# The w_lo subtraction of a split fp32 product moved from VectorE to GpSimd, with GpSimd's program planned by slots

## The reference, cut to what matters

```python
p = (rmsnorm(x, norm_w) * (1.0 + sc) + sh) @ w_in
pc = (rmsnorm(ctx, norm_w) * (1.0 + sc_c) + sh_c) @ w_in
qa, ka, va, za, qkvb, zb, ab = split_in(p)
y_a = diff_post(diff_attend_blocked(q_l, k_all, v_all, lam), subln_w, lam_init, za)
o_b, o_bc = delta_bidirectional(lat_in, ctx_in)
y_b = delta_post(o_b, dn_norm_w, zb)
x = x + gt * (jnp.concatenate([y_a, y_b], axis=-1) @ w_out)
```

## Time and profile before

| what | value |
|---|---|
| runs | 2801.6, 2807.7, 2818.62 us; median 2807.7 us |
| profiled execution, span | 2805.5 us |
| TensorE busy | 2441.5 us, 87% |
| DVE busy | 1479.5 us, 53%, 2582 instructions |
| ACT busy | 840.5 us, 30% |
| POOL busy | 335.5 us, 12%, 685 instructions |

### The profile page before, as it was taken

The page is one execution under the profiler, slowest core; times in us unless marked ns, Lnnn a source line. Parts: engine busy times, 40 slices in busy tenths (PEclk is TensorE's granted clock), DMA queues, the critical chain, the costliest instruction groups (busy, mean ns, idle before and its releaser), DMA issues. The chain is left out here.

```text
span 2805.5 us, 41589 instructions
## 1 busy us (share of the span) xinstructions
PE 2441.5 (87%) x15126; PEld 2006.7 (72%) x15126; DVE 1479.5 (53%) x2582; ACT 840.5 (30%) x1415; POOL 335.5 (12%) x685
## 2 busy tenths in 40 slices
PE   6799999999898989897898798988889898987776
PEld 2377778777776868685776476868777686866775
DVE  1345556473737373745433746475656656565535
ACT  3433232323223232323111533223232323223223
POOL 0001011111102020201100002020111202021100
PEclk9999999999999999998998699999999999998888
DMA  8945352626253544434334244443243444333433
GB/s 324 355 113 153 83 152 62 167 70 173 70 152 91 140 104 126 110 102 147 109 104 151 81 108 119 103 107 101 77 110 78 123 106 107 95 92 112 125 110 110
DMA packets 580888, 345.00 MB, mean 123 GB/s; under 512 B 45090, under 2 KB 544966, under 8 KB 579990
## 3 DMA queue, kind: packets, MB, share of 16 engines
q1 hardware_dynamic: 553430, 300.38, 38.7%
q10 hardware_dynamic: 27120, 42.02, 4.7%
q0 software_dynamic: 208, 0.72, 0.1%
HBM read 312.07 MB, written 31.00 MB: 122 GB/s over the span
## 5 line engine op out<-in xcount | busy, mean ns | idle before, releaser
L1604 PE MATMUL ps<-h_hi,w_hi 128*128 128x512 f32 (+1 forms) x2080 | 846.7, 407 | 49.2 <-DVE w_lo L972 38.1
L1605 PE MATMUL ps<-h_lo,w_hi 128*128 128x512 f32 (+1 forms) x2080 | 780.5, 375 | 0.0
L1606 PE MATMUL ps<-h_hi,w_lo 128*128 128x512 f32 (+1 forms) x2080 | 779.6, 375 | 0.0
L972 DVE TENSOR_TENSOR w_lo<-w_raw,w_hi 128x1024 fp32r<-128x1024 f32 (+1 forms) x332 | 405.4, 1222 | 329.7 <-ACT w_hi L569 270.0
L1604 PEld LDWEIGHTS ps<-h_hi,w_hi 128*128 128x128 f32 x2080 | 407.6, 196 | 166.5 <-issue 64.4
L569 ACT CAST w_hi<-w_raw 128x1024 fp32r<-128x1024 f32 (+1 forms) x332 | 340.6, 1029 | 522.0 <-PE ps L1606 197.5
L1606 PEld LDWEIGHTS ps<-h_hi,w_lo 128*128 128x128 f32 x2080 | 407.1, 196 | 70.0
L1605 PEld LDWEIGHTS ps<-h_lo,w_hi 128*128 128x128 f32 x2080 | 409.4, 197 | 47.9
L1457 POOL TENSOR_SCALAR small<-small 128x4 f32<-128x4 f32 (+3 forms) x51 | 14.0, 274 | 2056.5 <-DVE small L1260 1018.1
L1854 PE MATMUL ps<-h_hi,w_hi 128*128 128x512 f32 (+1 forms) x448 | 169.7, 379 | 56.7 <-DVE w_lo L972 56.7
L972 DVE TENSOR_TENSOR arena<-arena,ps 128x512 f32<-128x512 f32 x160 | 104.1, 684 | 129.5 <-PE ps L1686 128.6
(11 more groups left out here) (187 smaller groups left out, 3164.0 us busy)
## 6 DMA issues: line engine op xcount, KB each, us to landing
w_raw<-in_w_in SPq DMA_DIRECT2D x260, 512.0 KB, 4.6
ada_raw<-in_w_ada SPq DMA_DIRECT2D x148, 512.0 KB, 5.4
w_raw<-in_w_out SPq DMA_DIRECT2D x64, 448.0 KB, 3.7
w_raw<-in_w_ada SPq DMA_DIRECT2D x44, 512.0 KB, 7.0
arena<-decay_rows ACTq DMA_DIRECT2D x16, 512.0 KB, 5.4
m_chunks<-arena SPq DMA_DIRECT2D x16, 512.0 KB, 5.5
arena<-s_chunks SPq DMA_DIRECT2D x16, 512.0 KB, 3.9
x_channel_major<-arena ACTq DMA_DIRECT2D x1, 4096.0 KB, 17.2
```

What stands on the lines that cost most here:

```text
L972: return V.tensor_tensor(o, a, b, op)
L1604: mm(o, w_hi[:, s, k], h_hi[:, kt, t0:], start=kt == 0, stop=False)
L1605: mm(o, w_hi[:, s, k], h_lo[:, kt, t0:], start=False, stop=False)
L1606: last = mm(o, w_lo[:, s, k], h_hi[:, kt, t0:], start=False, stop=kt == KT - 1)
```

## The change

split_lo goes from the DVE's program to POOL's, with the same operands and semaphores, as a tensor_tensor of POOL. All 332 subtractions go: the two and the one at each layer's start, those of slot 2, 6, 10 and so on of each body, those of the output product, and three of the last four units (the first of these belongs to the output body). POOL's body is now planned by slots as the others are: the power of q and k in slot 3, the products with the gates in slot 6, the memsets in slot 9, the forward substitution in five parts of three steps in slots 15 to 19, the output norms' powers in slot 36 (20 in layer 1) and 58. A subtraction stands ahead of what else is in its slot, in the output body behind it. TensorE's, ACT's and SP's programs are the same as before. On the DVE of layer 1 the modulation of the first 8 and the second 8 channel tiles is now one call, since no subtraction is between them.

```diff
@@ -1015,13 +1015,6 @@
                 vec.wait_ge(diag_ready, n + 1)
                 own.settle()
 
-            def split_lo(i, u, tiles=HALF):
-
-                vec.wait_ge(w_hi_ready, i * UNITS + (u + 1))
-                need(vec, w_used, i * UNITS + (u - 1))
-                tt(w_lo[:, u % 2, 0:tiles], w_raw[:, u % 4, 0:tiles], w_hi[:, u % 2, 0:tiles].bitcast(F32),
-                   ALU.subtract).then_inc(w_split, 1)
-
             def modulate(layer, ks):
 
 
@@ -1060,8 +1053,6 @@
                     rms(0, 0)
                 if g == 2:
                     vec.wait_ge(rms_copied, 1)
-                if g == 7:
-                    split_lo(0, 0)
                 q = modulated_after(g)
                 if q >= 0:
                     modulate(0, range(4 * q, 4 * q + 4))
@@ -1071,14 +1062,9 @@
                 c0 = first_q(layer)
                 own.finish()
                 if layer:
-                    split_lo(0, base)
                     rms(layer, 0)
                     vec.wait_ge(rms_copied, layer + 1)
-                    modulate(layer, range(HALF))
-                    split_lo(0, base + 1)
-                    modulate(layer, range(HALF, KT))
-                else:
-                    split_lo(0, base + 1)
+                    modulate(layer, range(KT))
 
                 vec.wait_ge(x_stored, 16 * (1 + layer * KT))
                 own.done(V.memset(cin, 0.0))
@@ -1385,11 +1371,7 @@
                         put(62, y_lo_last, 1)
                         for n in range(KT):
                             put(out_slot(n), part_add, n)
-                        for u in range(OUT_UNITS):
-                            put(piece_slot(2 * u), split_lo, 0, first + u + 1, OUT_HEADS if u < OUT_UNITS - 1 else HALF)
                     for s in range(SLOTS):
-                        if project and s % 4 == 2:
-                            split_lo(i, base + 2 + s // 4 + 1)
                         for f, a in plan.get(s, ()):
                             f(*a)
                     own.finish()
@@ -1408,7 +1390,6 @@
                     if c0 == 0:
                         own.settle()
 
-                split_lo(0, base + 2)
                 own.finish()
                 heads(vec, layer, body)
 
@@ -1422,8 +1403,6 @@
 
                 for n in range(KT):
                     if n % 4 == 0:
-                        if n // 4 + 1 < LAST_UNITS:
-                            split_lo(0, first + OUT_UNITS + n // 4 + 1)
                         vec.wait_ge(old_loaded[n // 4], 16 * (layer + 1))
 
                     vec.wait_ge(last_product, layer * KT + n + 1)
@@ -1462,51 +1441,93 @@
                 pool.wait_ge(sums_copied, n) if n else pool.wait_ge(x_measured, NT)
                 power(small[:, 44 + c0:48], small[:, 44 + c0:48], NT - c0, 1.0 / D, NORM_EPS, rms_ready, n + 1)
 
+            def split_lo(i, u, tiles=HALF):
+
+                pool.wait_ge(w_hi_ready, i * UNITS + (u + 1))
+                need(pool, w_used, i * UNITS + (u - 1))
+                G.tensor_tensor(w_lo[:, u % 2, 0:tiles], w_raw[:, u % 4, 0:tiles], w_hi[:, u % 2, 0:tiles].bitcast(F32),
+                                ALU.subtract).then_inc(w_split, 1)
+
             for layer in range(DEPTH):
+                base = layer * LAYER_UNITS
+                first = base + 2 + HEADS * UNITS
                 c0 = first_q(layer)
                 own.finish()
                 rms(layer, 0)
+                for u in range(3):
+                    split_lo(0, base + u)
 
                 def body(i, project, fill):
                     own.finish()
-                    if not fill:
-                        return
 
                     def h(off=-1, per=1, idx=1):
                         return nth(layer, i, off, per, idx)
 
-
-                    pool.wait_ge(qk_summed, h())
-                    power(small[:, 8 + c0:16], small[:, c0:8], 8 - c0, 1.0, 4e-6, qk_rms, h())
-
-                    pool.wait_ge(qk_normed, h())
-                    need(pool, w_product, h(-2, 2, 2))
-                    need(pool, s_product, h(-2, 3, 3))
-                    for d in range(2):
-                        for n, dst in ((TAB_GROW, k_grow), (TAB_END, k_end)):
-                            m = G.tensor_tensor(dst[:, d], qk_tok[:, NT:], hcol[:, n, d].unsqueeze(2).to_broadcast([P, NT, P]),
-                                                ALU.mult)
-                            if (d, n) != (1, TAB_END):
-                                own.go(m)
-                    m.then_inc(k_scaled, 1)
-                    own.settle()
-                    pool.wait_ge(k_scaled, h())
-
-                    own.done(G.memset(blk_s, 0.0))
-                    G.memset(blk_s[:, 0::BLK + 1], 1.0).then_inc(blk_identity, 1)
-                    pool.wait_ge(blk_identity, h())
-                    pool.wait_ge(blocks_in, h(-1, 16, 16))
-                    substitute(G, own, 0, range(BLK - 1))
-                    pool.sem_inc(blocks_solved, 1)
-
-                    pool.wait_ge(oa_summed, h())
-                    power(small[:, 28 + c0:32], small[:, 24 + c0:28], NT - c0, 1.0 / P, SUBLN_EPS, oa_rms, h())
-                    pool.wait_ge(ob_summed, h())
-                    power(small[:, 20 + c0:24], small[:, 16 + c0:20], NT - c0, 1.0 / P, NORM_EPS, ob_rms, h())
+                    def qk_power():
+                        pool.wait_ge(qk_summed, h())
+                        power(small[:, 8 + c0:16], small[:, c0:8], 8 - c0, 1.0, 4e-6, qk_rms, h())
+
+                    def k_scale():
+                        pool.wait_ge(qk_normed, h())
+                        need(pool, w_product, h(-2, 2, 2))
+                        need(pool, s_product, h(-2, 3, 3))
+                        for d in range(2):
+                            for n, dst in ((TAB_GROW, k_grow), (TAB_END, k_end)):
+                                m = G.tensor_tensor(dst[:, d], qk_tok[:, NT:], hcol[:, n, d].unsqueeze(2).to_broadcast([P, NT, P]),
+                                                    ALU.mult)
+                                if (d, n) != (1, TAB_END):
+                                    own.go(m)
+                        m.then_inc(k_scaled, 1)
+                        own.settle()
+                        pool.wait_ge(k_scaled, h())
+
+                    def identity_blocks():
+                        own.done(G.memset(blk_s, 0.0))
+                        G.memset(blk_s[:, 0::BLK + 1], 1.0).then_inc(blk_identity, 1)
+                        pool.wait_ge(blk_identity, h())
+
+                    def substitute_forward(n):
+                        if n == 0:
+                            pool.wait_ge(blocks_in, h(-1, 16, 16))
+                        substitute(G, own, 0, range(3 * n, 3 * n + 3))
+                        if n == 4:
+                            pool.sem_inc(blocks_solved, 1)
+
+                    def oa_power():
+                        pool.wait_ge(oa_summed, h())
+                        power(small[:, 28 + c0:32], small[:, 24 + c0:28], NT - c0, 1.0 / P, SUBLN_EPS, oa_rms, h())
+
+                    def ob_power():
+                        pool.wait_ge(ob_summed, h())
+                        power(small[:, 20 + c0:24], small[:, 16 + c0:20], NT - c0, 1.0 / P, NORM_EPS, ob_rms, h())
+
+                    plan = {}
+
+                    def put(s, f, *a):
+                        plan.setdefault(s, []).append((f, a))
+
+                    if fill:
+                        put(3, qk_power)
+                        put(6, k_scale)
+                        put(9, identity_blocks)
+                        for n in range(5):
+                            put(15 + n, substitute_forward, n)
+                        put(4 + 8 * len(q_tiles[layer]), oa_power)
+                        put(58, ob_power)
+                    if not project:
+                        for u in range(OUT_UNITS):
+                            put(piece_slot(2 * u), split_lo, 0, first + u + 1, OUT_HEADS if u < OUT_UNITS - 1 else HALF)
+                    for s in range(SLOTS):
+                        if project and s % 4 == 2:
+                            split_lo(i, base + 2 + s // 4 + 1)
+                        for f, a in plan.get(s, ()):
+                            f(*a)
                     own.finish()
 
                 own.finish()
                 heads(pool, layer, body)
+                for u in range(1, LAST_UNITS):
+                    split_lo(0, first + OUT_UNITS + u)
 
             own.finish()
             rms(DEPTH, N_CTX // P)
```

## The result

| | before | after |
|---|---|---|
| median of 8 runs | 2812.19 us | 2823.73 us |
| ratio to before | 1 | 1.0047 (95% interval 1.0033 to 1.006) |
| profiled execution, span | 2805.5 us | 2817.2 us |

The change makes the kernel slower by about 11.5 us. It is under 1%, so on the scale of the prediction "no change"; but the forecast was 29 us faster, and the interval leaves no doubt of the sign.

A forecast was written before the change was run, and what follows sets the result against it. It took TensorE's own work (busy 2441.5 of 2805.5 us) plus 364 us idleness as the bound. Stage terms, chiefly -48 in layer 1's later heads against +9 and +15.6 in output parts, summed to -28.7: 2778 us, range 2728 to 2832.

The forecast's parts named there:

- the 2.05 that was to be the sign: New profile: POOL's w_lo subtraction was to show a minimum near 2.05 us, its price where the DVE stands idle.
- case D: Rival, chance 0.18: POOL's subtraction on the path and blocked DVE taps and additions make the kernel slower, +41 us, 2849.
- about 80: Output parts: TensorE's waits on w_lo were to rise from 56.7 to about 80 us.
- the -48: Later heads of layer 1: summed forecast gain, -6.85 us per head times 7.
- (1): Later heads of layer 1, first query tile's mix: no subtraction ahead, so its wait goes, -3.75 us per head.
- (2): Later heads of layer 1, second tile's mix: the subtraction ahead of it is gone, -0.9 us per head.
- (3): Later heads of layer 1: substitution starts 3 us earlier, so a unit waits 0.9 instead of 2.89: -2.0 us per head.
- (4): Later heads of layer 1, rest of a head: short waits for a late subtraction go, -1.1 us per head.
- (5): Later heads of layer 1: subtractions with little behind them cost +0.4 near the head's start, +1.3 after late weight loads.
- (6): Later heads of layer 1: shorter gaps give back granted clock, -0.8 us per head.
- case B: Rival, chance 0.17: mutual blocking costs the DVE little, layer 0's later mixes come early too; -79 us, 2729.
- C: Rival, chance 0.19: layer 1 gains, but the substitution's gain fails (+14) and output parts cost more (+9): -6, 2802.

## Why the prediction was wrong

It said 2778 us, faster, and the kernel after takes 2823.73 us, inside the range of 2728 to 2832 and on the other side of before. By stage, 23.1 of the 40.4 us between forecast and measurement lie in the later heads of layer 1, 9.4 in those of layer 0, 4.3 in the bare heads, 2.5 in the last units, 0.9 in the output products, and 0.2 in start and boundary.

**Price: wrong.** "I take 2.05 where the DVE stands idle": it is 2.34 there (the row I took, has a broadcast operand, which I did not weigh). In the kernel it is 2448 ns on average for 128x1024 and 2097 for 128x896. On the path a subtraction costs 1.1 us more than the DVE's for 1024 columns and 2.10 - 1.10 = 1.0 for 896, not 0.8 and 0.7. The estimate by the Trainium skill, GPSIMD Engine Reference, section 3 (2.25 against 1.15), came nearer than the row; its 1.1 us more is what was measured. The minimum of all, 2070 ns, looks like the 2.05 that was to be the sign, but it is the 896-column form. The threshold of case D, "a mean of 2.43 us takes the whole gain", was worked out for 1024 columns, and 2448 ns is over it. With D's count of 75 on the path, 28 of them of 896 columns, the price alone takes 47 x 0.40 + 28 x 0.28 = 27 of the 28.7 us; that is an estimate, and the count was too high, as the output products show.

**Output products: the mechanism right, the sum right by luck.** +24.6 forecast, +25.5 measured, waits on w_lo 79.4 us where "about 80" stood. The price was too low and the count of 28 on the path too high by about as much: 22.7 us more of waits at 1.0 each are 23. The run with half the columns shows that it is length alone.

**Later heads of layer 1: half of the -48, and half of that half is the clock.** This is the largest miss. (1) holds: of the 3.75 us at the first mix nothing is left. (2) fails: the second mix waits 0.99 us, all that it had (0.98). (3) fails. Timeline of one such head after:

```profile
2104.47 2.63 POOL L1448 TENSOR_TENSOR w_lo<-w_raw,w_hi 128x1024 fp32r<-128x1024 f32 x1 [2.23 <-ACT w_hi L569]
2107.05 4.04 POOL L1476 TENSOR_TENSOR arena<-arena,hcol 128x512 f32<-128x512 f32 x4
...
2111.92 2.39 POOL L1448 TENSOR_TENSOR w_lo<-w_raw,w_hi 128x1024 fp32r<-128x1024 f32 x1 [0.22 <-POOL arena L1486]
...
2115.03 0.52 SPq L507 DMA_DIRECT2D m_chunks<-arena  x1
...
2130.44 2.34 POOL L1448 TENSOR_TENSOR w_lo<-w_raw,w_hi 128x1024 fp32r<-128x1024 f32 x1 [0.22 <-POOL arena L289]
...
2132.84 0.68 PE L1625 MATMUL ps<-h_hi,w_hi 128*128 128x512 f32 x1 [2.85 <-POOL w_lo L1448]
```

I had POOL do the subtraction of unit 3 as soon as its cast was there. It stands behind the subtraction of unit 2, which waits for its own cast, then behind the four products: one engine, in order, nearly 10 us from 2104.47 to the end of unit 3's. So the store still waits for the subtraction of unit 3, the substitution does not begin 3 us sooner, and unit 5 waits 2.7 us in the mean of the seven heads, where it had waited 2.9. (The text's 0.9 us for it is short by its own numbers too: 2116.6 - 2116.29 + 0.9 is 1.2.) (4) and (5): the short waits for w_lo, 1.3 us per head before, did not go but grew to 4.4: 1.28 us at unit 1, 1.13 at unit 2, 0.48 at unit 6 and 0.75 at unit 11 in this head, 1.10 at unit 12 in most others. I had 1.7 in all. (6) is the other way: TensorE's busy time fell by 1.7 us per head, not 0.8. The stage gives 3.6 us per head, not 6.85, and only 1.8 of them are idle time.

**Later heads of layer 0: the wrong side.** I had the second mix blocked at its own instruction and the third unchanged. What is blocked is the tap ahead of it, by the whole of POOL's subtraction. In the mean of the seven heads that costs 1.6 us at the third mix (2.9 in the head shown, 5.84 against 2.95), a little more than the first two gave (0.8 and 0.5). The run with the taps moved shows that it is this and not the exponentials, which was my argument against case B. I had this mutual blocking in the text as an open size and gave it 2 us once per head; over the kernel it is 193 us on the DVE. The mix makes 2.4 of the stage's 5.9 us; waits on ACT's copy L718 (3.7 us, none before) are the next part and stay open.

**Bare heads.** +8.4 instead of +4.1. The waits on w_lo there rose from 2.8 to 9.3 us, in 7 waits where there were 6: too cheap, and too few.

**Last units.** -4.4 instead of -6.9: right mechanism, size off. The wait of 2.02 us is 1.24, not "gone but for a few tenths". The DVE is not held by its own subtraction any more; what else holds its additions stays open.

The sign has no single cause. With the taps moved behind the mixes the time ends 0.17% below before (0.9983); the order of work on POOL in layer 1 and the price are then still in it, and the forecast gain does not come back. Of the signs that it named, the waits on the mix came down from 85.7 to 68.1 us and not to 45. Of its own signs of being wrong one came: waits on POOL's w_lo beyond 2 us in the middle of heads, at unit 5 of every head of layer 1 (2.3 to 3.7 us).

Of the rivals C is nearest in time: it had (3) not paying, and said -6; but its +9 on the output products did not come, and it left out layer 0. D had the sign and named the taps being blocked, with the subtraction on the path too long as well, and made it +41; the additions, which it also named, were not blocked.

## What to carry to other kernels

Price an instruction on another engine from a row with the same operands, not only the same operation: a broadcast operand made POOL's row 17% too cheap (1.04 against 1.26 us). Follow the receiving engine's own program as well: in order, each piece waits for the casts and products of the pieces ahead of it. Moving work off the DVE to POOL gave back about half of what it freed (193 of 405 us), since DVE instructions that read SBUF stood still beside it, so look at what stands in front of the waiting instruction while POOL runs, and put there operations with an operand in PSUM, which were not held. And move only those units whose consumer is far: where the operation follows its producer on the path the slower engine's length is the price, at every one.

## What the runs showed of the hardware

- POOL's tensor_tensor with two full operands of 1024 fp32 columns: 2.34 us alone, with a broadcast second operand 1.90; for 512 columns 1.26 and 1.04. The output type does not matter.
- A DVE instruction that has only one operand in SBUF, but copies or multiplies from SBUF to SBUF, is held by POOL's subtraction as well (1.93 and 1.92 us instead of 0.43 alone for the tensor_scalar), down to one of 128x4 (up to 2256 ns instead of 170).
- POOL's memset, which only writes, held the small tensor_scalar too: two of 128x4 took 1.18 us beside a memset of 0.95. A tensor_tensor with two SBUF operands kept its 0.69 beside a memset, in an overlap of 0.24 us only.
- DVE instructions with one operand in SBUF and one in PSUM were not held: 0.69 and 0.75 in the pairs, and in the kernel 96 additions of 481 ns before and after the change.
- Of the 405.3 us that left the DVE, 193 came back as longer instructions, while POOL was busy with subtractions for 790.2 us. If all of the 193 is blocking, about a quarter of POOL's time held the DVE.
- The same 15126 TensorE instructions were busy 2441.5 us before and 2427.4 after, at mean granted clocks of 0.939 and 0.945: why the clock was granted higher was not tried.
